# Attention of a two-layer decoder step: the product of weights and values issued for four key blocks at a time instead of two

## The reference

```
s = einsum('bqhd,bkhd->bhqk', q_i, k) * ATTN_SCALE
s = s + cq_i[..., :, None] - ck[:, :, None, :]
p = softmax(where(key_pos <= q_pos, s, -inf), axis=-1)
out = einsum('bhqk,bkhd->bqhd', p, v)
```

## Time and profile before

| | us |
|---|---|
| median of the runs | 3304.84 |
| profiled execution | 3305.91 |
| its span | 3304.3 |
| TensorE busy in the span | 2939.4 |
| attention stage, from the first maximum's product to the last store | about 1945 to 3062 |
| mean granted TensorE clock in the span | 0.93 of full speed |

### The profile page before, as it was taken

The page is one execution under the profiler, slowest core; times in us unless marked ns, Lnnn a source line. Parts: engine busy times, 40 slices in busy tenths (PEclk is TensorE's granted clock), DMA queues, the critical chain, the costliest instruction groups (busy, mean ns, idle before and its releaser), DMA issues. The chain is left out here.

```text
span 3304.3 us, 46930 instructions
## 1 busy us (share of the span) xinstructions
PE 2939.4 (89%) x17133; PEld 2242.9 (68%) x17133; DVE 1599.6 (48%) x2148; ACT 1032.1 (31%) x1721; POOL 1376.5 (42%) x986
## 2 busy tenths in 40 slices
PE   3888787877888998979999859999999999999899
PEld 3878786866676998878999835454444545444787
DVE  4232323243454778986555454445545454543432
ACT  4322222222344222221112114444444444434200
POOL 0000000001001676667888736676666665657000
PEclk9998998988998999989999959899999998989899
DMA  4101010106554788878777668686776866864532
GB/s 119 34 20 39 21 38 20 38 13 201 173 157 133 241 270 269 277 256 273 254 253 254 205 151 228 171 237 178 207 223 177 235 175 186 228 161 150 176 115 72
DMA packets 327904, 547.51 MB, mean 166 GB/s; under 512 B 76093, under 2 KB 220129, under 8 KB 319212
## 3 DMA queue, kind: packets, MB, share of 16 engines
q1 hardware_dynamic: 263564, 471.12, 48.7%
q10 hardware_dynamic: 61120, 58.83, 5.1%
q0 software_dynamic: 3008, 14.81, 1.3%
HBM read 449.58 MB, written 95.12 MB: 165 GB/s over the span
## 5 line engine op out<-in xcount | busy, mean ns | idle before, releaser
L1151 POOL TENSOR_TENSOR p_kp<-p_kp,p_qb 128x1024 f32<-128x1024 f32 x256 | 625.6, 2470 | 388.4 <-DMA p_kp<-in_cache_k_dram 307.4
L1992 POOL TENSOR_TENSOR at_acc<-at_acc,at_w 128x512 f32<-128x512 f32 (+3 forms) x576 | 643.2, 1117 | 305.5 <-ACT at_w L2120 247.4
L2152 DVE TENSOR_REDUCE at_mx<-at_mx 128x1 f32<-128x512 f32 (+3 forms) x640 | 383.0, 607 | 538.5 <-PE at_mx L2027 406.9
L112 PE MATMUL p_pb<-p_w,x_xh 128*128 128x256 f32 x2048 | 592.5, 289 | 8.9 <-DVE p_w L1465 8.9
L113 PE MATMUL p_pb<-p_w,x_xh 128*128 128x256 f32 x2048 | 579.9, 283 | 0.0
L114 PE MATMUL p_pb<-p_w,x_xl 128*128 128x256 f32 x2048 | 579.5, 283 | 0.0
L2120 ACT ACTIVATE at_w<-at_st,c_nckt 128x512 f32<-128x512 f32 (+3 forms) x640 | 397.4, 623 | 553.8 <-PE at_st L2053 306.1
L1567 DVE TENSOR_REDUCE p_sc<-p_kp 128x16 f32<-128x1024 f32 x256 | 307.9, 1215 | 221.6 <-POOL p_kp L1151 221.6
L112 PEld LDWEIGHTS p_pb<-p_w,x_xh 128*128 128x128 f32 x2048 | 391.4, 191 | 20.3 <-issue 10.6
L113 PEld LDWEIGHTS p_pb<-p_w,x_xh 128*128 128x128 f32 x2048 | 392.8, 192 | 0.0
L114 PEld LDWEIGHTS p_pb<-p_w,x_xl 128*128 128x128 f32 x2048 | 392.2, 191 | 0.0
(11 more groups left out here) (293 smaller groups left out, 3849.9 us busy)
## 6 DMA issues: line engine op xcount, KB each, us to landing
p_kp<-in_cache_k_dram SPq DMA_DIRECT2D x256, 512.0 KB, 5.0
at_vp<-in_cache_v_dram SPq DMA_DIRECT2D x256, 512.0 KB, 5.3
o_mt<-mixed SPq DMA_DIRECT2D x32, 512.0 KB, 5.6
p_raw<-in_w_in_dram SPq DMA_DIRECT2D x32, 512.0 KB, 7.4
at_q<-qh SPq DMA_DIRECT2D x32, 512.0 KB, 10.6
at_k<-kh SPq DMA_DIRECT2D x32, 512.0 KB, 8.7
l_raw<-in_w_in_dram SPq DMA_DIRECT2D x20, 512.0 KB
mixed<-l_w POOLq DMA_DIRECT2D x8, 1028.0 KB, 4.2
```

The lines of the kernel that those rows point to most:

```text
L112: nc.tensor.matmul(out, lhs[0], rhs[0], start=(k == 0), stop=False)
L1151: nc.gpsimd.tensor_tensor(kp[:, g % 4], kp[:, g % 4], qb[:], ALU.mult).then_inc(kmul, 1)
L1992: nc.gpsimd.tensor_tensor(t[:, 512 - wd:512], t[:, 512 - wd:512], W[n % RW][:, 0:wd], ALU.add).then_inc(accd, 1)
L2152: nc.vector.reduce_max(mx[:, u % 2, j, seg:seg + 1], MX[r % 2][:, 0:wd], AX.X).then_inc(mread, 1)
```

## The change

PV is issued for four key blocks in a row (`G = 4`) instead of two. A PV enters the list two steps after its last block, as before; the first of its blocks is then five steps old, where it was three. To hold the weights so long, `RW` goes from 6 to 8 buffers. `LEAD` goes from 20 to 22, `MR` stands three steps behind the unit's last maximum instead of two, and `OF` four steps behind the unit's last PV instead of two. All waits on `pv` count groups of four.

```diff
-    RW = 6
-    LEAD = 20
+    RW = 8
+    LEAD = 22
     NA = 6
+    G = 4
...
-            if kb == blocks(u) - 2:
+            if kb == blocks(u) - G:
                 seq.append(("OE", u))
...
-                        turn_at.setdefault(n + 2, []).append(v)
-                if kb % 2:
-                    pending.append((u, kb - 1, n - 1))
-                if pending and pending[0][2] + 1 <= n - 2:
+                        turn_at.setdefault(n + 3, []).append(v)
+                if kb % G == G - 1:
+                    pending.append((u, kb - G + 1, n - G + 1))
+                if pending and pending[0][2] + G - 1 <= n - 2:
                     p = pending.pop(0)
                     weigh(p)
-                    if p[1] == blocks(p[0]) - 2:
-                        later.setdefault(n + 2, []).append(("OF", p[0]))
+                    if p[1] == blocks(p[0]) - G:
+                        later.setdefault(n + 4, []).append(("OF", p[0]))
...
-                    sp.wait_ge(pv, first_step(NC * (h - 1)) // 2)
+                    sp.wait_ge(pv, first_step(NC * (h - 1)) // G)
...
-                    pe.wait_ge(ex, n + 2)
+                    pe.wait_ge(ex, n + G)
...
-                    for x in range(2):
+                    for x in range(G):
                         wd, y = width(n + x), HD * (x % 2)
...
-                        act.wait_ge(pv, (n - RW) // 2 + 1)
+                        act.wait_ge(pv, (n - RW) // G + 1)
...
-                    act.wait_ge(pv, (first_step(u) + blocks(u)) // 2)
+                    act.wait_ge(pv, (first_step(u) + blocks(u)) // G)
```

## The result

The changed kernel takes 3204.8 us (median of 4), against 3309.2 for the kernel before: ratio 0.969, 95% interval 0.962 to 0.976.

The account below looks back on a forecast made before the run. TensorE's instruction queue was taken to bound the attention stage. 61 us saved less 5 of burst waits gave 56, trimmed to 54 for the unseen: 3306 - 54 = 3252 us; own range 3236 to 3276, over the cases 3208 to 3296.

Parts of the forecast that it names:

- the clock's mean in the steady part: TensorE in the attention stage: the mean granted clock should stay near 0.94; a change of several per cent fails the prediction.
- The joined PV: Within the PV run: four products in a row take about 1.86 us against 2.02, 0.16 less per run.
- the rival in which the third product waits for its weights: In the PV run: four products still take 2.02 us, 26 us of gain are missing, 3278 us; chance 0.12.
- The whole term at full clock: TensorE within, behind and ahead of PV: 0.38 us saved for each of 160 runs, 61 us.
- the burst's waits: QK waiting for ScalarE's exponential in the four-step burst: 0 to 0.1 us, taken as 0.03, 160 times, 5 us.
- The first half of QK: Directly behind PV: it takes 0.33 us against 0.24 for the second half, 0.10 lost per PV run.
- M and its mask product: Ahead of PV: 0.21 us lost at M or 0.09 at the mask product, taken as 0.12 per run.
- that `OF` is covered by the PV: VectorE's `OF`, about 1.5 us, stands ahead of the burst's last M, and the PV behind covers it.
- the slower rival: ScalarE becomes the bound if `OE` and the row's copy don't hide: 91 us against 61, 3336 us; chance 0.06.
- GpSimd and the eight buffers: GpSimd may fall seven steps behind, costing nothing; the 10.9 us ScalarE waited for it go without gain.
- The samples' steps: Samples' first ten steps: `SA` waits 0.9 us, 4 us more in all; `SX` waits 0.6 less, 5 us in all.
- the waits go too: TensorE's 25.6 us of waits mostly vanish, with stretches at half clock: 3200 to 3235 us; chance 0.22.

Follow-up runs that it names:

- fours_light: The change with lighter VectorE work (31 of 33 pages of the samples' sums and 504 of 512 gate columns left out); ratio 0.966 to the kernel before.
- pairs_light: The kernel before with lighter VectorE work (31 of 33 pages of the samples' sums and 504 of 512 gate columns left out); ratio 0.987 to the kernel before.
- before_sums_later: The kernel before with the samples' product of sums `SX` and what follows it two steps later; ratio 0.987 to the kernel before.
- pairs_rest_kept: The change with `G` back from 4 to 2 and everything else kept; ratio 0.990 to the kernel before.
- fours_halves_early: The change with only `OF`, the halves' sum, moved back from four to two steps behind the last product; ratio 1.010 to the kernel before.
- fours_sums_early: The change with `SX` moved to the step of the reduction it needs, so that TensorE must wait; ratio 0.978 to the kernel before.

## Why the prediction was wrong

The step that failed is the clock's, in the sum and in the list of what would show it: "12% of the time is at half speed; I count half as much again there, 6% of 61, or 3 us", and "the clock's mean in the steady part should stay near 0.94". The runs showed 0.98, and 55 us where I had 3. I priced the removed pieces at the lower clock, but took the time at that clock as given. The range had the same fault: the ends of its own terms, taken all one way, reach down to 3223, not 3236, and still don't reach the measured 3205. By the split, the rest of the sum was too high by 12 us, which hid a part of what the clock brought.

Point by point:

- **The joined PV:** right. 1.87 against 1.86; the rival in which the third product waits for its weights is out.
- **The whole term at full clock:** right in kind, sized too high. Without the clock's 3 us the sum had 61 - 3 - 5 = 53 (160 times 0.38, less `VN`, less the burst's waits); the stage has 41 less. fours_light against pairs_light gives 28, with 8 us more in waits, so some 36 without. Adding up the start-to-start times by line, at full clock, shows where. From PV's start to the next product the stage has 27 us less (forecast 26). The first half of QK has 7 less (forecast 16): the third QK of a burst stands where a PV stood before it, and still takes 0.34 in some 55 of the 160 bursts, where its weights come late, and 0.32 in some 60 more, where the row's turn is now just ahead of it. I had given this place 0.03 us of wait, and the engine hardly waits there (0.5 us in all). M and its mask product have 7 less (forecast 19): the entries to the strips cost what I read, but the samples' turn now stands behind an M, which takes some 1.27 us to the turn's start in place of 0.24, some 8 us in eight samples, part of which stood behind PV before.
- **VectorE:** that `OF` is covered by the PV held for the change as it is. I didn't see that this was the whole condition: with `OF` two steps earlier the change is a loss of 1%. I had ScalarE as the slower rival; in no run did TensorE's matmuls wait for it more than 0.5 us at a time or 1.3 us in all in the steady part. The place to look was the two-deep ring of `MX`.
- **GpSimd and the eight buffers:** right; the 10.9 us that ScalarE waited for GpSimd before are gone, and no such wait is left in the steady part.
- **The samples' steps:** right, 5.9 and 4.1 us where I had 0.9 and 0.6 each time.
- **The rival "the waits go too"** named the right size, 3200 to 3235, and perhaps half of the reason. Its condition failed: the waits stayed at 23.5 us. But the long one at `SX`, on which it rested, did shrink from up to 1.3 us to 0.6, and the time at the lower clock in the samples' first steps fell from 72 to 17 us. How much of that is due to this wait is open: before_sums_later is without it and gained 1.3%, pairs_rest_kept still has it and stands at 10 us there. The other half, behind `VA` and at the stage's start, it didn't have.

Shown: the fours with the rest in place lower the time at the lower clock, with the waits (135 to 68 us) or with few (158 to 53); many waits of 1 to 2 us (fours_halves_early) or a few of 3 us (fours_sums_early) raise it. Not shown: which property of the fours does it, fewer passages into and out of the column strips or longer unbroken stretches of full-width products. No run separates these.

## What to carry to other kernels

Where TensorE is the bound, count its start-to-start times at each passage between full-array and column-strip products: joining two PV saved 0.15 us in the run and about 0.1 on either side. Then look at what comes to stand where the passage was: here the product in that place kept most of its extra 0.1. When a burst on one engine grows, look in every other engine's order for the long operation that now falls inside the burst, and move it to the step that the long run covers. Treat the share of time at the lower clock as something the change moves, with its own term and bounds on both sides, and not as a constant of the stage.

## What the hardware showed that I had not expected

TensorE's granted clock stayed at half for 23.8 us in which the profile has the engine busy throughout (pairs_light). In the kernel before it fell within 2 us behind each of the eight `VA`. A tiny product moved by two steps changed a kernel's time by 1.3% (before_sums_later), with 3 us less in waits. And a QK product took 0.34 us in place of 0.23 behind a wait that is nearly nothing; its weight load had not started ahead of it.
